# RMSNorm factors by a constant 128x128 matrix, ScalarE's inverse root and a Newton step on VectorE

## What is computed

```python
def rmsnorm(x, g):
    xf = x.astype(jnp.float32)
    y = xf * lax.rsqrt(jnp.mean(xf * xf, axis=-1, keepdims=True) + NORM_EPS)
    return (y * g.astype(jnp.float32)).astype(x.dtype)

hp = rmsnorm(xp, g_pre_mix[l])
xp = xp + rmsnorm(mp, g_post_mix[l])     # mp: the attention's output
xp = xp + rmsnorm(squared_relu_mlp(rmsnorm(xp, g_pre_ffn[l]), w_ffn_up[l], w_ffn_down[l]), g_post_ffn[l])
```

## Time and profile before

| | |
|---|---|
| Time, median of 3 executions | 2812.97 us (2811.93 to 2816.13) |
| The profiled execution, first to last instruction | 2812.3 us; which of the times is its own isn't marked, so the span is compared with the median, 0.7 us above it |
| PE busy | 2769.3 us, 98% of the span |
| DVE, ACT, POOL busy | 50%, 32%, 20% |
| Granted TensorE clock, mean | 0.996 |

### The profile page before, as it was taken

How to read it: one execution, slowest core, us unless ns; L and a number is a source line. 1 busy time by engine, 2 the same in 40 slices (tenths; PEclk the granted TensorE clock), 3 DMA queues, 4 the chain that set the end, 5 groups by cost and what they waited for, 6 DMA issues and landing times.

```text
span 2812.3 us, 49103 instructions
## 1 busy us (share of the span) xinstructions
PE 2769.3 (98%) x18736; PEld 2673.9 (95%) x18736; DVE 1409.7 (50%) x3191; ACT 889.2 (32%) x1671; POOL 568.6 (20%) x371
## 2 busy tenths in 40 slices
PE   8999999999999999999999999999999999999997
PEld 8999989899999999999989999988999999999997
DVE  6766666657333333333576666665653333333335
ACT  5444444544011111111453344345522111111114
POOL 1111100452121212112320000005412121212124
PEclk9999999999999999999999999999999999999999
DMA  5411211442111111111241111123411111111113
GB/s 182 144 60 59 72 72 71 141 169 79 53 38 52 37 52 37 52 36 53 77 159 62 62 61 62 70 93 121 169 70 38 53 37 52 37 52 37 52 38 127
DMA packets 59159, 210.46 MB, mean 75 GB/s; under 512 B 7016, under 2 KB 16624, under 8 KB 55840
## 3 DMA queue, kind: packets, MB, share of 16 engines
q1 hardware_dynamic: 55648, 174.64, 17.9%
q0 software_dynamic: 3408, 34.42, 3.0%
HBM read 163.36 MB, written 51.97 MB: 77 GB/s over the span
## 4 chain that ended last, share of the span: by engine, by line
PE 92%; DVE 3%; issue 2%; ACT 1%; POOL 1%; DMA 0%; SPq 0%; DVEq 0%; ACTq 0%; POOLq 0%
PE ps L1527 77%; PE ps L1662 4%; PE ps L1684 4%; PE ps L1623 2%; PE ps L1680 1%; PE ps L1633 1%; PE ps L1635 1%; DVE XL L1100 1%; DVE ACC L1091 1%; PE ps L1514 1%; POOL RB L631 0%; PE ps L1507 0%; DVE WL L1134 0%; PE ps L1645 0%; ACT XH L764 0%
## 5 line engine op out<-in xcount | busy, mean ns | idle before, releaser
L1527 PE MATMUL ps<-XH,WH 128*128 128x384 f32 (+1 forms) x3096 | 1027.7, 332 | 18.0 <-DVE WL L1149 8.0
L1527 PE MATMUL ps<-XH,WL 128*128 128x384 f32 (+1 forms) x3096 | 1023.1, 330 | 0.0
L1527 PE MATMUL ps<-XL,WH 128*128 128x384 f32 (+1 forms) x3096 | 1018.8, 329 | 0.0
L1527 PE MATMUL ps<-U,WH 128*128 128x384 f32 (+1 forms) x3072 | 747.8, 327 | 0.0
L592 POOL TENSOR_TENSOR WL<-WS,WH 128x1024 fp32r<-128x1024 f32 x160 | 384.3, 2403 | 1741.7 <-ACT WH L735 1741.6
L1527 PEld LDWEIGHTS ps<-XH,WH 128*128 128x128 f32 x3096 | 583.9, 189 | 29.4 <-issue 26.5
L1527 PEld LDWEIGHTS ps<-XH,WL 128*128 128x128 f32 x3096 | 583.5, 188 | 11.5 <-issue 11.5
L1527 PEld LDWEIGHTS ps<-XL,WH 128*128 128x128 f32 x3096 | 584.2, 189 | 3.9 <-issue 3.9
L1527 PEld LDWEIGHTS ps<-U,WH 128*128 128x128 f32 x3072 | 540.7, 188 | 0.0
L1527 PE MATMUL ps<-U,WL 128*128 128x384 f32 (+1 forms) x1536 | 501.5, 326 | 0.0
L735 ACT CAST WH<-WS 128x1024 fp32r<-128x1024 f32 x208 | 216.8, 1045 | 645.6 <-PE ps L1527 640.3
(11 more groups left out here) (138 smaller groups left out, 2127.6 us busy)
## 6 DMA issues: line engine op xcount, KB each, us to landing
WS<-w_in SPq DMA_DIRECT2D x209, 512.0 KB, 4.4
k_out<-KT SPq DMA_DIRECT2D x16, 672.0 KB, 3.2
x_scr<-XRES POOLq DMA_DIRECT2D x6, 1536.0 KB, 5.4
v_out<-VT SPq DMA_DIRECT2D x16, 544.0 KB, 4.9
o_scr<-OT SPq DMA_DIRECT2D x14, 544.0 KB, 2.7
XRES<-x_scr POOLq DMA_DIRECT2D x4, 1536.0 KB, 7.7
BIAS<-nc_scr SPq DMA_DIRECT2D x8, 672.0 KB, 4.9
toep_scr<-rel_scr SPq DMA_DIRECT2D x1, 5120.0 KB, 23.0
```

Source lines behind the costliest of these rows:

```text
L1527: return pe.matmul(bank[:, 0:w], wt, xt, start=m == 0, stop=m == 3 * tiles - 1, skip_group_check=False)
```

## The change

The constant column and matrix of ones become a 128x128 matrix `mean` of 0.5/1024. One fp32 matmul of all 384 (or 320) tokens of a chunk puts half the mean of squares of each token on all partitions at once (it takes the place of stat; bc is gone). ACT then makes z = 1/sqrt(2*that + eps) into RB (`Abs_reciprocal_sqrt`) and squares it into ZZH (piece rq). DVE makes a Newton step with two instructions (piece st), so that RB holds minus the factor: the additions behind it become subtractions, and evictions multiply by -1. POOL has no pow. Post's multiplications read the factor from RB in SBUF, where they read the PSUM bank before. The ticks of the tables and the order in T0 are adapted, and in n=4 the last half of chunk 1's additions goes from DVE to POOL.

```diff
+    "act": dict(post_rq=(1.05, 6.05, 10.9), pre_hi0=(2.5, 6.9, 12.5), pre_sq0=(2.9, 6.95, 12.9), pre_hi1=(3.5, 8.1, 13.5),
+                pre_sq1=(3.9, 8.5, 13.9), pre_rq=(7.95, 12.6, 14.95)),
...
-        ident, ones = own("ident", [P, P]), own("ones", [P, P])
+        ident, mean = own("ident", [P, P]), own("mean", [P, P])
...
+        halfpow, eps = own("halfpow", [P, 1]), own("eps", [P, 1])
...
-        DG, z1 = place("DG", z1, [P, 2, 384])
+        ZZH, z1 = place("ZZH", z1, [P, 2, 384])
...
-                elif what in ("post_pow", "pre_pow"):
-                    j = JOBS.index((n, c, what[:-4]))
-                    pool.wait_ge(sem["st"], j + 1)
-                    wait(pool, "dg", j)
-
-                    pool.tensor_tensor(RS[:, :], ST[:, :], halfpow[:, :], ALU.pow).then_inc(sem["pw"], 1)
+                elif what == "post_a1":
+                    pool.wait_ge(sem["xs"], 2 * nth_of(n, c, "post") + 2)
+                    pool.wait_ge(sem[f"xl{c}"], 16 * n)
+                    pool.tensor_tensor(ct(ACC, c, 4, 4), ct(XH, c, 4, 4).bitcast(f32), ct(ACC, c, 4, 4), ALU.subtract).then_inc(sem["xu"], 1)
...
+            pool.memset(mean[:, :], 0.5 / D_MODEL).then_inc(sem["ones"], 1)
+            pool.memset(eps[:, :], EPS).then_inc(sem["ones"], 1)
...
-                if what == "pre_rb":
-
-                    j = JOBS.index((n, c, "pre"))
-                    act.wait_ge(sem["rb"], j + 1)
-                    act.copy(RB[:, CHUNKS[c][0]:CHUNKS[c][0] + w], ps[:, 6 + j % 2, 0:w]).then_inc(sem["rbc"], 1)
-                    return
-                if what.endswith("dg"):
-                    j = JOBS.index((n, c, what[:-3]))
-                    act.wait_ge(sem["pw"], j + 1)
-                    act.wait_ge(sem["rb"], j - 1)
-                    for q in range(-(-w // P)):
-                        v = min(P, w - q * P)
-                        ins = act.activation(DG[0:v, j % 2, q * P:q * P + v], ident[0:v, 0:v], ACT.Copy, scale=RS[0:v, q:q + 1])
-                    ins.then_inc(sem["dg"], 1)
+                if what.endswith("rq"):
+
+                    j, cols = JOBS.index((n, c, what[:-3])), slice(CHUNKS[c][0], CHUNKS[c][0] + w)
+                    act.wait_ge(sem["sta"], j + 1)
+                    act.activation(RB[:, cols], ps[:, 6 + j % 2, 0:w], ACT.Abs_reciprocal_sqrt, bias=eps[:, 0:1], scale=2.0).then_inc(sem["zr"], 1)
+                    act.wait_ge(sem["zr"], j + 1)
+                    wait(act, "rf", j - 1)
+                    act.activation(ZZH[:, j % 2, 0:w], RB[:, cols], ACT.Square).then_inc(sem["zs"], 1)
...
-                    dve.wait_ge(sem["sta"], j + 1)
-                    wait(dve, "pw", j)
-                    ins = dve.tensor_scalar(ST[:, 0:full], ps[:, 6 + j % 2, 0:full], 1.0 / D_MODEL, EPS, ALU.mult, ALU.add)
-                    if rest:
-                        ins = dve.tensor_scalar(ST[0:rest, full:full + 1], ps[0:rest, 6 + j % 2, full:full + 1], 1.0 / D_MODEL, EPS,
-                                                ALU.mult, ALU.add)
-                    ins.then_inc(sem["st"], 1)
...
+                    dve.wait_ge(sem["zs"], j + 1)
+                    dve.scalar_tensor_tensor(out=ZZH[:, j % 2, 0:w], in0=ps[:, 6 + j % 2, 0:w], scalar=0.5 * EPS, in1=ZZH[:, j % 2, 0:w],
+                                             op0=ALU.add, op1=ALU.mult).then_inc(sem["nu"], 1)
+                    dve.wait_ge(sem["nu"], j + 1)
+                    dve.scalar_tensor_tensor(out=RB[:, cols], in0=ZZH[:, j % 2, 0:w], scalar=-1.5, in1=RB[:, cols],
+                                             op0=ALU.add, op1=ALU.mult).then_inc(sem["rf"], 1)
...
-                        factor = ps[:, 6 + j % 2:7 + j % 2, 0:w].to_broadcast([P, 4, w])
-                        ins = dve.tensor_tensor(acc, acc, factor, ALU.mult)
+                        ins = dve.tensor_tensor(acc, acc, factor(c, 4), ALU.mult)
...
-                    dve.tensor_tensor(ct(XRES, c, 4 * h, 4), ct(XRES, c, 4 * h, 4), ct(ACC, c, 4 * h, 4), ALU.add).then_inc(sem["xu"], 1)
+                    dve.tensor_tensor(ct(XRES, c, 4 * h, 4), ct(XRES, c, 4 * h, 4), ct(ACC, c, 4 * h, 4), ALU.subtract).then_inc(sem["xu"], 1)
...
-                    pieces(2, "post_st")
                     pieces(1, "pre_lo0 pre_lo1")
                     empty_next(0, 1)
                     pieces(1, "pre_red0 pre_red1")
-                    pieces(2, "post_x0")
+                    pieces(2, "post_st post_x0")
...
-                    if j >= 2:
-                        pn, pc, pp = JOBS[j - 2]
-                        if pp == "post":
-                            pe.wait_ge(sem["xs"], 2 * nth_of(pn, pc, pp) + 2)
-                        else:
-                            pe.wait_ge(sem["rbc"], nth_of(pn, pc, pp) + 1)
-                    for q in range(-(-w // P)):
-                        v = min(P, w - q * P)
-                        ins = pe.matmul(ps[0:v, 6 + j % 2, q:q + 1], src[:, q * P:q * P + v], ones[:, 0:1], start=True, stop=True)
-                    ins.then_inc(sem["sta"], 1)
-                else:
-
-                    pe.wait_ge(sem["dg"], j + 1)
-                    for q in range(-(-w // P)):
-                        v = min(P, w - q * P)
-                        ins = pe.matmul(ps[:, 6 + j % 2, q * P:q * P + v], ones[0:v, :], DG[0:v, j % 2, q * P:q * P + v], start=True, stop=True)
-                    ins.then_inc(sem["rb"], 1)
+                    wait(pe, "nu", j - 1)
+                    pe.matmul(ps[:, 6 + j % 2, 0:w], mean[:, :], src, start=True, stop=True).then_inc(sem["sta"], 1)
```

More of the change, by code:

```diff
@@ L419, in norms_over @@
             n = 0 if first_attention.layer == 0 else 2
-            for name, each in (("hl", 2), ("ps", 1), ("rbc", 1)):
+            for name, each in (("hl", 2), ("ps", 1)):
                 wait(eng, name, each * (nth_of(n, 2, "pre") + 1))
+            eng.wait_ge(sem["rf"], JOBS.index((n, 2, "pre")) + 1)
             for c in range(3):
@@ L778, in _ @@
                 act.nop().then_inc(sem[name], 1)
-            act.wait_ge(sem["ones"], 1)
-            act.activation(stats[:, 13:14], ones[:, 0:1], ACT.Copy)
+            act.wait_ge(sem["ones"], 2)
+            act.activation(stats[:, 13:14], mean[:, 0:1], ACT.Copy)
             act.wait_ge(sem["gain"], 16)
@@ L1021, in _, with factor @@
         def _(dve):
+            def factor(c, k):
+                o, w = CHUNKS[c]
+                return RB[:, o:o + w].rearrange("p (k w) -> p k w", k=1).to_broadcast([P, k, w])
             def norm(n, c, what):
@@ L1025, in norm @@
                 j = JOBS.index((n, c, part))
-                full, rest = w // P, w % P
+                cols = slice(CHUNKS[c][0], CHUNKS[c][0] + w)
                 if step == "red0":
@@ L1108, in scaled @@
             def scaled(n, c):
-                dve.wait_ge(sem["rbc"], nth_of(n, c, "pre") + 1)
+                dve.wait_ge(sem["rf"], JOBS.index((n, c, "pre")) + 1)
             def empty_qkv(c, u, bank):
@@ L1179, in empty_start @@
                         else:
-                            dve.tensor_tensor(ZF[:, t0:t0 + w], ps[0:8, s % 6, 0:w], RB[0:8, t0:t0 + w], ALU.mult)\
-                                .then_inc(sem["evG"], 1)
+                            dve.scalar_tensor_tensor(out=ZF[:, t0:t0 + w], in0=ps[0:8, s % 6, 0:w], scalar=-1.0, in1=RB[0:8, t0:t0 + w],
+                                                     op0=ALU.mult, op1=ALU.mult).then_inc(sem["evG"], 1)
                     for s in range(4):
@@ L1186, in _ @@
                     statistics(2, "red0 red1")
-                    statistics(1, "dg")
+                    for s in range(4, 8):
+                        empty_start(s)
                     statistics(2, "st")
-                    for s in range(4, 7):
-                        empty_start(s)
-                    statistics(2, "dg")
-                    empty_start(7)
                     dve.wait_ge(sem["fl"], 80)
@@ L1550, in _ @@
                     if sec.layer == 0:
[L1551 to L1552 removed]
+                        at = {(2, 12): 0, (6, 0): 1, (8, 0): 2}
                         for s in range(12):
@@ L1594, in _ @@
                     if sec.g0 % GROUPS == 0:
-                        pe.wait_ge(sem["rbc"], nth_of(2 * sec.layer, 2, "pre") + 1)
+                        pe.wait_ge(sem["rf"], JOBS.index((2 * sec.layer, 2, "pre")) + 1)
                     with runs(pe, sec) as i:
```

101 lines of the change are left out of this document (42 added, 59 removed).

## The result

| | before | changed |
|---|---|---|
| Time, median | 2813.3 us (4 executions) | 2825.3 us (4 executions, 2822.48 to 2828.42) |
| Ratio, 95% interval | | 1.0042 (1.003 to 1.0055) |
| Profiled execution, span | 2812.3 | 2822.2 |
| PE busy | 2769.3 | 2750.7 |
| DVE busy | 1409.7 | 1442.9 |

The change costs 12 us, 0.4%. The forecast was 2816.4 in a range of 2800 to 2823, so the time lies outside, on the side of rival C. The miss is 8.9 us. The other 6.5 are in the span, which grew by 9.9 where +3.4 was forecast.

What follows compares the result with a forecast made beforehand. PE, busy 98%, bounds the kernel, its saving lost waiting for DVE: start -2.0, n=1 +1.0, n=3 +1.0, n=2 +0.4, n=4 +3.0, sum +3.4 on span 2812.3; median 0.7 above, 2816.4 us; range 2800 to 2823.

Steps and rivals of the forecast that it cites:

- rival C: DVE and POOL lock each other out at full price in n=1, n=3 and at the end: 2821.4 us, chance 0.28.
- The two norms n=1 and n=3: Later PSX sums from DVE make PE wait, less one stat saved behind each: +1.0 us in each norm.
- n=2: Where layer 1 begins, DVE's Newton step waits for ACT's rq and delays chunk 2's XL: +0.4 us, bounds -1 and +3.
- The bound and the meetings without slack: PE is busy 98%; sums are ready 0.24 us before PE wants them or later, so DVE's extra time is PE's loss.
- Rival B: PE's saving stands because DVE, busy for 50%, has room for 1 us a job: 2797 us, chance 0.24.
- PE's part: In all 24 jobs the new matmul costs a bc's 0.66 us and one stat of 0.67 goes: 16.1 us saved.
- Two inputs in SBUF: Eight multiplications in n=1 reading the factor from SBUF are blocked by POOL's WL: 1.2 x 2.41 = +2.9 us, bounds 0 and +4.8.
- The waits for chunks 1 and 2: FF group of n=1: two Newton steps of 1.06 us, less DVE's idle 1.38 and vanished writings 0.3, plus hand-overs 0.2: +0.65.
- The clock behind a wait: In n=2, PE's clock may stand at 1.2 instead of 2.4 GHz behind a longer stall: +0.7 us.
- n=4 up to the last stat: PE's saving for chunks 0 and 1 is lost again at the last stat, which waits for DVE's last output: -0.1 us.
- The end: After the last stat: stat to multiplication -0.5 us, one blocking of DVE by POOL's subtraction for its whole length +3.6.
- The table loads: ACT's table loads, eight instead of three, fall in its idle time: 0 us, bound 6.4, or 13.3 by the skill's figure.

Runs made afterwards that it cites:

- experiment 1: Changed kernel, with post's factor written back to its PSUM bank and read there by the multiplications: 2815.3 us, ratio to before 1.0004.
- experiment 2: Kernel before the change, with ACT copying chunk 0's post factor to RB in n=1 and n=3, where the eight multiplications read it: 2826.7 us, ratio 1.0044.
- 6: Kernel of 5, with DVE's two Newton instructions left out of every job, so the output's numbers differ: 2790.9 us.
- 7: Kernel of 5, chunk 2's Newton step moved behind chunk 1's PSX sums in n=1 and n=3: 2808.2 us; with two more changes of DVE's order: 2804.3 us.
- Experiment 3: Changed kernel, with one tick altered so that in n=2 ACT makes chunk 1's rq ahead of chunk 2's first half of XH: 2820.8 us.
- experiment 8: Last reordered kernel of 7, with the last half of chunk 1's subtraction in n=4 on POOL: 2802.7 us; unchanged, with it on DVE: 2803.3 us.
- 4: Changed kernel, with the last half of chunk 1's subtraction in n=4 back on DVE instead of POOL: 2825.7 us.
- 5: Changed kernel with the edits of experiment 1, Experiment 3 and 4 together: 2808.4 us, ratio 0.998 to the kernel before.

## Why the prediction was wrong

Three terms of the sum failed, all of them sizes of waits on PE for DVE. The two norms n=1 and n=3 had +1.0 each and gave +3.9 and +3.8, and n=2 had +0.4 and gave +4.7: 10.0 us too little in all. The other rows of the table went the other way, by 3.5 in all: 0.5 at the start, 1.6 in attention, 1.7 in n=4, less 0.3 at the end. None of this was foreseen, so it is luck that the forecast was not further off.

**The bound and the meetings without slack** were read rightly: PE's busy time falls by 18.6 us, for 14 to 22 forecast, and none of it stays in the whole, because DVE decides at PSX in n=1 and n=3 and at XL in n=2. Rival B, which needed slack on DVE, fell.

**PE's part** was right: from its start to that of the product behind it the new matmul takes 0.35 us and the product behind it 0.29 more than its pace, 0.64 together, against the 0.66 taken. n=0 gave -2.5 for -2.0, which says little: the ten experiments' profiles have -1.3 to -4.3 there, and the -1.3 is of the kernel before with its n=0 unchanged.

**Two inputs in SBUF** is the step that failed first: the mechanism was right, its size not. I took 1.2 blockings (+2.9), and it was +4.5, near rival C's price; experiment 1 gives 10 us for it over the whole program and experiment 2 puts 13.5 on the kernel before with it and the copy that it needs there. The gain set against it, a factor 1.2 us earlier, was 1.0 (3.21 us from the stat's start at 596.07 to the first multiplication, for 4.17 from 600.22 in the kernel before). The Trainium skill ("SBUF — State Buffer", the section on its two sides) says that the loser is blocked for the other's whole instruction. The rows agree (one multiplication of each four ends 0.4 us behind the WL beside it, POOL's WL is longer where it starts second, and a factor in PSUM ends it), and by that rule at full price, one blocking for each group of four, +4.8, the term would have been nearly right.

**The waits for chunks 1 and 2** failed too: I let DVE's idle 1.38 us and the vanished writings of `factors` absorb most of the two Newton steps (+0.65), and PE waited 1.63 and 2.02 there. Experiments 6 and 7 show it: without the step these waits are gone (0.27 us is left), and with the step moved alone the same wait stands elsewhere. With the sums moved too, the two waits come to 1.85 us instead of 3.43, so that part of it was order; the rest DVE has no room for in any order tried.

**The clock behind a wait** was in the sum only once, with 0.7. After 3.38 us of waiting in n=1 PE had 0.56 of its clock for 3.8 us, about 1.6 us lost (matmuls of 384 columns 0.32 apart instead of 0.17, and two longer ones ahead), and after 6.28 us in n=2 0.50 for 4.3, about 2. A new wait of this length on PE cost its length and this; behind the waits of 1.63 and 2.02 us in the changed kernel's n=1 the clock stayed full, and behind the same 2.02 us in experiment 1's profile (at 679.50) it fell to half for 3.4 us.

**n=2** was forecast with +0.4 and gave +4.7. The place, the order and the 3 us (DVE's wait was 3.02) stood in the prediction; the step that failed is that DVE would make up for most of the 3.9 us by 1449.16. XL came at 1452.9, 3.9 late: the whole sum. In the kernel before DVE stood idle there for 0.54 us only the earlier trace rows, so there was nothing to make it up with. Experiment 3 gives 4.5 us for the order alone.

**n=4 up to the last stat** gave -1.8 for -0.1. The prediction let PE lose its saving again in the wait for DVE's last output. But this output stands behind PE's last product (DVE waits for PE ahead of its last eviction in both kernels, 0.57 and 0.42 us, at 2794.84 and 2801.24), so it comes earlier with PE, and the wait stays as it was, 3.01 us for 2.86.

**The end** was right in place, and its size in part by luck (+3.1 forecast, +3.4 in the row "from there to the end"). The first small multiplication starts 4.51 us behind the stat instead of 5.58, which is 1.1 gained for 0.5; DVE's instruction was blocked for 3.1, for 3.6; and from DVE's last instruction to the end of the span, in which the last store lands, are 3.9 us instead of 2.6, which was not in the sum. The reservation under experiment 8 holds for all of it. **The table loads** cost nothing in n=1, as taken: the load runs from 595.50 to 596.78, and the matmul that its root needs ended at 596.88; in n=3 it is the same. In n=0 one load lies in the way of its root (26.62 to 27.91, the root starts at 27.92), and no loss is seen behind it. From the end of the instruction ahead (26.61) to the root are 1.31 us, so this switch costs the load alone, and nothing here speaks for the larger bound of 13.3.

Rival C was the nearest, 2821.4, with the right mechanism. (By the prediction's own prices the full blocking is +2.9 in n=1 and n=3, not +2.5, which makes C 2822.2.) It lacked the clock, chunks 1 and 2, and n=2: its 2.5, 2.5 and 0.4 stand against 3.9, 3.8 and 4.7, and its 5 at the end against 3.4. The same three terms are the reason why 2823 was too low an upper end.

## What to carry to other kernels

Work taken from the engine that bounds a kernel is a gain only as far as the engine that it meets has slack; where a sum is ready 0.2 us before it is wanted, a microsecond put on its engine had its full price here, and behind a wait of 3 us a stretch at half the clock as well. Before an operand is moved from PSUM to SBUF on DVE, look at what POOL does in that stretch. When a new piece waits in an in-order queue, look for idle time ahead of the piece that it stands behind: here one tick was worth 4.5 us of 2825.

## What I had not expected of the hardware

The same wait of 1.62 us left PE's clock at 2.4 GHz in one execution and at 1.2 for 3 us in another, which cost 1.6 us. Such chances go with the spread of one kernel's executions: of the 24 of the kernel before that ran beside experiments 1, 3, 4 and 5, the four with a mean granted clock of 0.994 took 2815.8 to 2816.3 us, the fifteen with 0.996 took 2811.0 to 2814.8. That is more than most single edits are worth. In the meetings of DVE and POOL POOL is longer as well (3.94 us for a WL of 2.41), so that both lose: each waits when it is the second to start.
